# Gate and up of six feed-forward stages with x stationary and 512 weight columns moving; their product turned in 32x32 blocks on VectorE and moved between quadrants by ScalarE's DMAs

## The reference

```python
def rmsnorm(x, g):
    x32 = x.astype(jnp.float32)
    y = x32 * lax.rsqrt(jnp.mean(x32 * x32, axis=-1, keepdims=True) + EPS)
    return y.astype(x.dtype) * g

def swiglu(x, w_gate, w_up, w_down):          # 1024 -> 2816 -> 1024
    return (jax.nn.silu(x @ w_gate) * (x @ w_up)) @ w_down

x = x + 0.5 * swiglu(rmsnorm(x, ffn1_norm[l]), ffn1_w_gate[l], ffn1_w_up[l], ffn1_w_down[l])
```

## Time and profile before

| | us |
|---|---|
| median of 3 runs | 1545.18 (1545.06 to 1545.27) |
| span of the profiled execution, first to last instruction | 1543.2 |
| PE busy | 1533.1 (99%) |
| DVE busy | 1111.1 (72%) |
| ACT busy | 833.6 (54%) |
| DMA bytes | 282.46 MB, mean 183 GB/s |

### The profile page before, as it was taken

How to read it: one execution, slowest core, us unless ns; L and a number is a source line. 1 busy time by engine, 2 the same in 40 slices (tenths; PEclk the granted TensorE clock), 3 DMA queues, 4 the chain that set the end, 5 groups by cost and what they waited for, 6 DMA issues and landing times.

```text
span 1543.2 us, 23159 instructions
## 1 busy us (share of the span) xinstructions
PE 1533.1 (99%) x8920; PEld 1335.5 (87%) x8920; DVE 1111.1 (72%) x1568; ACT 833.6 (54%) x1168; POOL 83.8 (5%) x195
## 2 busy tenths in 40 slices
PE   9999999999999999999999999999999999999998
PEld 7888899988888888889988888888888997888886
DVE  6687779667666776666756876678766789876676
ACT  6565456555445555455555654455555564554555
POOL 0500002000000000000000081000000000000000
PEclk9999999999999999999999999999999999999999
DMA  8865653546555565554535556546655473655551
GB/s 303 237 227 193 192 164 137 191 137 205 203 190 171 165 218 182 196 189 163 175 123 164 188 166 214 190 141 205 217 190 176 149 219 100 212 196 197 190 191 55
DMA packets 207585, 282.46 MB, mean 183 GB/s; under 512 B 5578, under 2 KB 179528, under 8 KB 207512
## 3 DMA queue, kind: packets, MB, share of 16 engines
q1 hardware_dynamic: 202880, 274.51, 53.3%
q0 software_dynamic: 1584, 3.83, 0.9%
q10 hardware_dynamic: 3048, 3.11, 0.8%
HBM read 279.92 MB, written 3.08 MB: 183 GB/s over the span
## 4 chain that ended last, share of the span: by engine, by line
PE 97%; DVE 1%; ACT 1%; DMA 0%; issue 0%; SPq 0%; DVEq 0%; ACTq 0%
PE bank L1758 44%; PE bank L1809 32%; PE bank L1808 14%; PE bank L1811 2%; PE bank L1886 1%; PE bank L2048 1%; PE bank L2019 1%; PE bank L2277 1%; PE bank L2037 1%; DVE w_lo L1104 0%; DMA x<-in_x 0%; PE bank L1927 0%; PE bank L2027 0%; DVE arena L1701 0%; DVE x L1702 0%; ACT arena L1037 0%
## 5 line engine op out<-in xcount | busy, mean ns | idle before, releaser
L1104 DVE TENSOR_TENSOR w_lo<-raw,w_hi 128x1024 fp32r<-128x1024 f32 x514 | 615.4, 1227 | 213.3 <-ACT w_hi L612 212.8
L1809 PE MATMUL bank<-xT,w_hi 128*128 128x512 f32 x2112 | 733.6, 397 | 0.0
L612 ACT ACTIVATE w_hi<-raw 128x1024 fp32r<-128x1024 f32 x514 | 526.7, 1051 | 153.4 <-PE bank L1809 79.0
L1808 PE MATMUL bank<-xT,w_lo 128*128 128x256 f32 x1848 | 516.7, 280 | 0.0
L1809 PEld LDWEIGHTS bank<-xT,w_hi 128*128 128x128 f32 x2112 | 383.3, 188 | 73.5 <-DVE w_lo L1104 0.3
L1808 PEld LDWEIGHTS bank<-xT,w_lo 128*128 128x128 f32 x1848 | 348.6, 189 | 12.1 <-DVE w_lo L1386 0.3
L1758 PE MATMUL bank<-w_hi,hid_hi 128*128 128x512 f32 x524 | 205.7, 393 | 0.0
L1758 PE MATMUL bank<-w_hi,hid_lo 128*128 128x512 f32 x524 | 204.4, 390 | 0.0
L1758 PE MATMUL bank<-w_lo,hid_hi 128*128 128x512 f32 x524 | 204.2, 390 | 0.0
L1758 PE MATMUL bank<-xT,w_hi 128*128 128x256 f32 x816 | 148.7, 285 | 0.0
L1758 PEld LDWEIGHTS bank<-xT,w_hi 128*128 128x128 f32 x816 | 127.7, 192 | 0.9 <-issue 0.3
(11 more groups left out here) (301 smaller groups left out, 1519.3 us busy)
## 6 DMA issues: line engine op xcount, KB each, us to landing
raw<-in_ffn_w_down SPq DMA_DIRECT2D x44, 1024.0 KB, 5.5
raw<-in_ffn_w_in SPq DMA_DIRECT2D x44, 1024.0 KB, 5.1
raw<-in_ffn_w_gate SPq DMA_DIRECT2D x43, 1024.0 KB, 5.4
raw<-in_ffn_w_up SPq DMA_DIRECT2D x43, 1024.0 KB, 5.4
raw<-in_ffn_w_out SPq DMA_DIRECT2D x22, 1024.0 KB, 5.3
raw<-in_w_in SPq DMA_DIRECT2D x10, 1024.0 KB, 5.2
raw<-in_xa_w_kv SPq DMA_DIRECT2D x8, 1024.0 KB, 5.2
raw<-in_od_w_in SPq DMA_DIRECT2D x8, 1024.0 KB, 5.5
```

The costliest lines, as they stand in the source:

```text
L612: act.activation(hi, src, ACT.Copy).then_inc(sem["hi_ready"], 1)
L1104: dve.tensor_tensor(lo, src, hi.bitcast(F32), ALU.subtract).then_inc(sem["lo_ready"], 1)
L1808: pe.matmul(bank[:, b, T:2 * T], lo, xT_hi[:, k, :], start=False, stop=False)
L1809: last = pe.matmul(bank[:, b, :], hi, xT[:, k, :, :], start=k == 0, stop=k == KD - 1)
```

## The change

An FFN is now cut in six *blocks* of 512 features, the last one of 256. A block takes eight halves: four of gate, four of up; then come four halves of down for the block before. In the last block, gate and up share four halves (256 columns each), then come four halves of down for block 4 and two for block 5. A weight half holds 2 k-tiles x 512 columns.

- Gate and up have the x tile stationary (`block_tile`, through `products`): twelve matmuls of 512 columns to a half. The result lies as tokens x features, gate in banks 0 and 1, up in 2 and 3. There is no right part to add, and 1/rms of a token is now a scalar per partition.
- ACT: silu reads the bank and scales by `rstd`. DVE: one instruction per 128 tokens makes up x rstd x silu(gate) (`hidden_product`). `scale_broadcast` and the diagonal are gone from the FFNs.
- Down needs the hidden features on the partitions. DVE transposes 32x32 blocks in place (`hidden_transposes`), and ACT issues 16 DMAs (`move_quadrants`), each of 32 partitions x 8 x 128 bytes (4 x 128 bytes in the last block), for each of 4x4 pairs of source and target quadrant. ACT then makes `hid_hi` from what has landed, DVE `hid_lo`.
- The work on the first half of x that precedes `rest_of_x` is now two full halves. In the fifth FFN `second_squares` stands ahead of the block's splits.
- The first halves of the program are loaded in other pieces; loads of gate and up are 4 k-tiles x 512 columns.

The diff at its core (line numbers left out):

```diff
@@ units
     def ffn_units(gate, up, down):
-        col_unit(gate, 0)
-        col_unit(up, 0)
-        for j in range(1, NJ):
-            col_unit(gate, j * UC)
-            col_unit(up, j * UC)
-            row_unit(down, (j - 1) * UC)
-        row_unit(down, (NJ - 1) * UC)
+        for k in (0, 4):
+            block_unit(gate, k, 0)
+            block_unit(up, k, 0)
+        for b in range(1, NB - 1):
+            for w in (gate, up):
+                for k in (0, 4):
+                    block_unit(w, k, b * BLOCK)
+            for r in (0, UC):
+                row_unit(down, (b - 1) * BLOCK + r)
...
@@ ScalarE
+            def ffn_block(f, b, i=None, first=None, after=None, opened=0):
...
+                def silu():
+                    act.wait_ge(sem["half_done"], plus(f.v0 + first_half(b) + gate_at, LOOP_HALVES))
...
+                    for t in range(NT):
+                        act.activation(act_gate[:, t, 0:n], bank[:, t, 0:n], ACT.Silu, scale=rstd[:, t:t + 1])\
+                            .then_inc(sem["gate_done"], 1)
+
+                def move_quadrants():
...
+                    act.wait_ge(sem["blocks_turned"], plus(f.b0 + b + 1, 1))
+                    for q in range(4):
+                        for c_ in range(4):
+                            act.dma_start(by_token[c_ * g:(c_ + 1) * g, q, 0:NT * n_tiles, :],
+                                          by_block[q * g:(q + 1) * g, c_, 0:NT * n_tiles, :]).then_inc(sem["hid_T_ready"], 16)
+
+                def hidden_high(tiles, src_tiles):
+                    act.wait_ge(sem["hid_T_ready"], plus(256 * (f.b0 + b + (1 if b == NB - 1 and tiles.start else 0)), 256))
+                    act.activation(hid_hi[:, tiles, :], hid_T[:, src_tiles, :], ACT.Copy).then_inc(sem["hidden_hi_ready"], 1)
+
+                if first is not None:
+                    first()
+                for n in range(n_splits):
+                    if n == gate_at:
+                        silu()
                     split(i, base + n)
...
+                    if n == 0 and b:
+                        hidden_high(slice(0, 4), slice(0, 4))
+                    if n == 4 and b == NB - 1:
+                        move_quadrants()
+                    if n == 5 and b == NB - 1:
+                        hidden_high(slice(4, 6), slice(0, 2))
+                    if n == 9 and 0 < b < NB - 1:
+                        move_quadrants()
+                if b == 0:
+                    move_quadrants()
@@ VectorE
+            def hidden_product(f, b, i):
...
+                    dve.scalar_tensor_tensor(hidden[:, t, 0:n], up, rstd[:, t:t + 1], act_gate[:, t, 0:n],
+                                             ALU.mult, ALU.mult).then_inc(sem["hidden_ready"], 1)
...
+            def hidden_transposes(b):
...
+                for t in range(NT):
+                    last = dve.transpose(out_of[:, t, 0:n_tiles], src[:, t, 0:n_tiles])
+                last.then_inc(sem["blocks_turned"], 1)
...
+                if b == NB - 1:
+                    for n in range(1, 4):
+                        split(i, base + n)
+                    hidden_product(f, b, i)
+                    hidden_transposes(b)
+                    split(i, base + 4)
+                    hidden_low(f, b, i)
+                    for n in range(5, 8):
+                        split(i, base + n)
...
+                    add_residual(0.5, between=lambda: split(i, base + 8))
@@ TensorE
+                def block_tile(v, b, t, k, kk):
+                    return products(bank[:, b + t, :], tuple(m[:, k, t * P:(t + 1) * P] for m in X), w_cols(v, kk, 512),
+                                    k == 0, k == KD - 1)
+
+                def block_half(v, b, n, i=None):
+                    split_ready(v, i)
+                    for t in range(NT):
+                        for kk in range(2):
+                            last = block_tile(v, b, t, 2 * n + kk, kk)
+                    last.then_inc(sem["half_done"], 1)
```

More of the change, by code:

```diff
@@ L1268, in ffn_step @@
-                if after_hidden is not None:
-                    after_hidden()
-                if j == NJ - 1:
-                    split(i, base + 5)
-                    add_residual(0.5, between=lambda: split(i, base + 6))
-                else:
-                    for n in range(4, n_splits):
+                    hidden_product(f, b, i)
+                    hidden_transposes(b)
+                    for n in range(8, n_splits):
                         split(i, base + n)
+                if after is not None:
+                    after()
@@ L1959, in down @@
+                def down(b, i=None, v=None, between=None):
+                    ready = b0 + b + 1
+                    pe.wait_ge(sem["hidden_lo_ready"], ready if i is None else ready + i)
+                    if b == NB - 1:
+                        last_rows(v, HID, 4)
                         return
-                    for s in range(2):
-                        row_half(v + s, d_bank, HID, 2 * (j % 2) + s, j == 0 and s == 0, False, i)
-                        if s == 0 and between is not None:
+                    for s in range(4):
+                        row_half(v + s, d_bank, HID, s, b == 0 and i is None and s == 0, False, i)
+                        if s == 1 and between is not None:
@@ new lines, in first_halves @@
+                def first_halves(n_half):
+                    v = v0 + n_half
+                    n, b = 2 * (n_half // 4) + n_half % 2, 2 * (n_half // 2 % 2)
+                    if first_transposes is not None and n_half == 0:
+                        pe.wait_ge(sem["first_lo_ready"], 1)
+                    else:
+                        split_ready(v, None)
+                    for t in range(NT):
+                        for kk in range(2):
+                            if b == 0 and t == 0:
+                                c.next("xT_lo_ready")
+                            if first_transposes is not None and (n_half, t, kk) == (0, 0, 1):
+                                split_ready(v, None)
+                            last = block_tile(v, b, t, 2 * n + kk, kk)
+                    last.then_inc(sem["half_done"], 1)
@@ L1994, in ffn @@
+                for n in range(8):
+                    if n == 2:
+                        if first_transposes is not None:
+                            first_transposes(2)
+                            first_transposes(3)
+                        else:
+                            rest_of_x()
+                    first_halves(n)
                 if late:
```

528 lines of the change are left out of this document (207 added, 321 removed).

## The result

The changed kernel takes 1631.88 us (median of 4 runs, 1626.27 to 1633.14), the kernel before beside it 1545.22 us (1545.06 to 1545.60): ratio 1.0552, 95% interval 1.0536 to 1.0569. It is slower, as forecast, but by 86.7 us where I had said 18.4, and outside my range. The profiled execution took 1631.74 us, with a span of 1630.0.

What follows compares the result with a forecast made beforehand. PE was taken as the bound, busy 99% of the span. -18.4 (gain) + 19.8 (A) + 8.6 (B) + 4.6 (C) + 1.8 (D) + 2.0 (E) = +18.4 us on 1545.2: 1563.6 us, range 1543 to 1592.

Steps and rivals of the forecast that it cites:

- A: Last block of each FFN: PE waits 3.3 us for `hid_lo` behind sixteen DMA issues; six times, 19.8 us (12.6 to 31.8).
- the clock: Rival, chance 0.10: PE's clock falls to half speed once in each FFN, costing 10.5 us; time 1574 us.
- the gain: Gate and up halves with fewer matmuls save 17.7 us, the dropped broadcasts 0.7; 18.4 us in all.
- no gain: Rival, chance 0.02: old and new gate and up forms cost alike per column; time 1581 us.
- E: Behind block 0 in five FFNs: PE waits 0.4 us for half 14's low part; 2.0 us in all (0 to 10).
- weight loads have slack: Weight loads land after 5.5 us, and ACT waited 4.2 us at most for one tensor; no cost counted.
- D: First FFN, behind block 0: ACT's two squares of the memory stand ahead of half 13's split; 1.8 us.
- B: Behind the last block's `hid_lo`: PE waits 1.4 us for the first residual, behind three low splits; six times, 8.6 us.
- C: Fifth FFN: PE waits 3.9 us before the sixth half, then 0.7 more for the next split; 4.6 us.
- Slow packets: Rival, chance 0.10: the moves land in 7.1 us, as the 263 KB ones; +63 us, time 1609 us.
- Covered: Rival, chance 0.13: DMA issues are quick enough that the last block's waits vanish; faster, time 1533 us.
- draw: Rival, chance 0.07: issues at 0.3 us and quick landings; A about 0.5 us, B 1.4; time 1545 us.

## Why the prediction was right or wrong

The direction was right, and so was most of the list of places. The forecast failed at two steps. One is the price of an issue between SBUF places, 0.48 us taken and 0.65 measured, on which A rested and the "It just fits" behind block 0; the waits there came to 32.9 and 24.0 us where the sum had 19.8 and 2.0. The other is the clock, which the sum left out on the ground that PE is never idle that long, and which cost 34.1 us, half of the 68 us by which the forecast was off.

- **Which view, and the gain: right.** PE bounded the kernel; 18.4 us forecast, 22.7 measured (20.1 from the iteration for 17.7, 2.6 for the broadcasts for 0.7). The rival *no gain* is out.
- **A, the wait for `hid_lo`: place and cause right, size short.** 19.8 us forecast, 32.9 measured, 5.5 each for 3.3. The mis-sized term is the issue: 0.48 us taken, 0.65 measured. Fifteen of them make 9.8 for 7.2, so +2.6. The moves started 0.9 us later (3.4 behind down's start, for 2.5), since ACT's and DVE's splits stood ahead of silu and product. Landing was 2.0 for 3.0. I had bounded the price by the earlier trace rows, two rows 0.05 apart that both had DRAM at one end; no SBUF to SBUF issue stood in the trace, and I took a narrow bracket of near rows for a bound. The end for A, 5.3 a time, was below what came.
- **E, behind block 0: of the waits, the step that failed most.** 2.0 us forecast, 24.0 measured (4.86, 5.12, 4.93, 4.82, 4.24). I had written "It just fits", with 0.7 us of room, and costed what comes behind it. Two things used the room: the burst, 3.1 us longer up to the split behind it, and the first issue, 2.4 us later than the 3.0 I had counted (table load, weights, two low splits ahead of the product). Together 5.5, and 4.9 us of wait. That *weight loads have slack* was wrong here too: ACT waited 5.10 us for one load, where the earlier trace rows had 4.2 for all loads of a tensor. A step that fits by 0.7 us behind sixteen terms of one price has a range of sixteen times that price's error; I gave it 0 to 10 for the landing and nothing for the issues.
- **D: direction right, short.** 1.8 us forecast; 5.9 measured in the first FFN. Two more waits there had no term at all: 3.0 at 85.8 behind the moves of block 1, where I had written "nothing" for the middle blocks, and 2.1 for silu.
- **B: right as a mechanism, hidden in the changed kernel.** 8.6 us forecast, none measured (the 0.5 us in the view of waits stands in the kernel before as well), as PE ran its two groups at half speed. Without the slow clock it is 4.6 to 5.5 us.
- **C: right.** 3.6 us for 3.9 at the sixth half; the further 0.7 did not show. But taking it away did not give it back.
- **The clock: the rival had the mechanism and a wrong size.** I priced it at 1.75 us, six times, 10.5 us, and gave it a chance of 0.10 as an alternative. It is 34.1 us, behind each of this kernel's fifteen waits of 2 us and more, 2.3 each, and it comes on top of the waits, not instead of them. The stretch in the earlier trace rows is cut off by the end of the program; inside they last 3.4 us or 6.8. And "never that long in my numbers" rested on the 3.3 us of A, whose own end was 5.3.
- *Slow packets*: out. The 32 KB moves land in 2.0 us (median), and the 147,432 packets of their queue take 7.4% of the DMA engines' time, 0.013 us a packet where I had taken 0.065 as the far end. The Trainium skill (DMA: Bandwidth & Descriptors, "Why small descriptors are slow (HBM only)") had this case fall away, and it does; but by bytes the packets are not free of a penalty: 0.36% of the engines' time for a MB, against 0.18% in the weights' queue. *Covered* and *draw* are out.

The errors did not fall together by chance: the burst is a term of A, D and E, and each of these waits then buys half-speed time. How much of the 68 us is due to the 0.17 us an issue alone, no run shows; halving the number of issues gave back 77.

## What to carry to other kernels

An engine that issues a burst of DMAs is busy for the whole burst: price it, where both ends lie in SBUF, as count x 0.65 us of that engine (measured here), then ask what stands behind it in the same queue, and let the count be the first thing to cut. Where PE is the bound, a wait of several us costs its length and often half-speed work behind it (here 34.1 us on 73.1); sum the waits first and put the clock on top of them, not beside them as a rival. Where several steps rest on one unmeasured price, move it to its far end in all of them together before giving a range.

## What the runs showed of the hardware

- Sixteen small DMAs between SBUF places took 10.1 to 10.6 us to issue on ACT alone, 10.1 and 10.5 on SP, 5.5 when split over both; the Trainium skill (DMA: Bandwidth & Descriptors, "Issuing engines are not separate DMA queues") grants a second engine just that, the time to initiate, and calls it usually small beside the DMA itself. Here it isn't: ten us of issuing for 2.0 us of landing.
- With the DMA engines at 0.99 the same burst took 16.07 us.
- Filling matmuls in a wait made the kernel 12.7 us faster than the changed one (1619.2 for 1631.9).
- At half clock 512-column matmuls started 0.43 us apart, at full clock 0.227.
- Half-speed stretches came behind fifteen waits of PE of 2.06 to 5.89 us in the changed kernel, but not behind one of 3.26 us with eight moves.
